# The order of requests in an attention, and the order of the first tiles, in a hybrid decoder block on one Trainium2 core

## What is computed

```python
u = rms_norm(h, norm_w[layer])
proj = jnp.einsum('bsd,dc->bsc', u, w_in[layer])
hg_q, hg_f, hg_i, hg_z, at_q, at_k, at_v, at_z = jnp.split(proj, split_points, axis=-1)
o_hg = hgrn2_mixer(hg_q, hg_f, hg_i, lb)                      # gated linear recurrence
o_hg = rms_norm_per_head(o_hg) * g * silu(hg_z)
q, k = rope(at_q, positions), rope(at_k, positions)
for window, dilation in ((128, 1), (512, 4), (2048, 16)):     # causal, dilated windows
    outs, lses <- dilated_window_attention(q, k, at_v, window, dilation)
o_at = sum(softmax(lses) * outs) * silu(at_z)
h = h + concat([o_hg, o_at]) @ w_out
return rms_norm(h, final_norm_w)
```

## Time and profile before

| | us |
|---|---|
| median of 3 runs (1322.99, 1329.15, 1329.57) | 1329.15 |
| the profiled execution, its own time | 1334.47 |
| its span, first to last instruction | 1332.7 |
| TensorE busy, share of the span | 1278.8, 96% |
| VectorE, ScalarE, GpSimd busy | 702.9, 462.8, 435.6 |

### The profile page before, as it was taken

One profiled execution on the slowest core, in us unless ns is written; L12 is line 12 of the kernel. 1 busy time (PEld: TensorE's weight loads), 2 busy tenths in 40 slices (PEclk: granted clock), 3 DMA queues, 4 the chain that ended last, 5 costly groups with the idle time before them and its releaser, 6 DMA issues.

```text
span 1332.7 us, 23441 instructions
## 1 busy us (share of the span) xinstructions
PE 1278.8 (96%) x8520; PEld 1111.0 (83%) x8520; DVE 702.9 (53%) x1885; ACT 462.8 (35%) x1328; POOL 435.6 (33%) x441
## 2 busy tenths in 40 slices
PE   5999999999999999999999999999999998999997
PEld 5989988999999989999878777877788776878886
DVE  5846776676666668310444544454455445433332
ACT  6721222121222212112445544554555456311111
POOL 5732344232533323030233333333433333202000
PEclk9999999999999999999999999999999999999999
DMA  6520112211121122233355445544554666545431
GB/s 219 157 84 16 58 61 74 72 57 56 56 71 53 61 88 64 61 113 84 83 145 138 121 107 145 138 120 109 152 139 113 163 179 167 168 136 172 143 111 63
DMA packets 121714, 143.89 MB, mean 108 GB/s; under 512 B 20352, under 2 KB 86400, under 8 KB 121600
## 3 DMA queue, kind: packets, MB, share of 16 engines
q1 hardware_dynamic: 119200, 138.46, 36.7%
q10 hardware_dynamic: 2400, 3.93, 1.2%
HBM read 87.56 MB, written 29.62 MB: 88 GB/s over the span
## 4 chain that ended last, share of the span: by engine, by line
PE 79%; DMA 9%; DVE 4%; SPq 2%; issue 2%; POOL 2%; ACT 1%; ACTq 0%; POOLq 0%; DVEq 0%
PE bank L657 11%; PE bank L659 10%; PE bank L658 10%; PE bank L849 4%; PE bank L851 4%; PE bank L850 4%; PE bank L822 4%; PE bank L823 4%; PE bank L821 4%; DMA ks<-turned 3%; PE bank L913 2%; PE bank L982 2%; PE bank L922 2%; PE bank L738 2%; PE bank L975 2%
## 5 line engine op out<-in xcount | busy, mean ns | idle before, releaser
L657 PE MATMUL bank<-w_hi,u_hi 128*128 128x256 f32 x768 | 220.9, 288 | 1.5 <-POOL w_lo L1263 1.0
L659 PE MATMUL bank<-w_hi,u_lo 128*128 128x256 f32 x768 | 217.8, 284 | 0.0
L658 PE MATMUL bank<-w_lo,u_hi 128*128 128x256 f32 x768 | 217.7, 283 | 0.0
L657 PEld LDWEIGHTS bank<-w_hi,u_hi 128*128 128x128 f32 x768 | 147.5, 192 | 3.2 <-DVE u_lo L1442 1.7
L658 PEld LDWEIGHTS bank<-w_lo,u_hi 128*128 128x128 f32 x768 | 147.6, 192 | 0.1
L659 PEld LDWEIGHTS bank<-w_hi,u_lo 128*128 128x128 f32 x768 | 147.5, 192 | 0.1
L1442 DVE TENSOR_TENSOR room<-room 128x256 f32<-128x256 f32 (+6 forms) x386 | 133.7, 394 | 14.7 <-POOL room L1327 7.8
L1442 DVE TENSOR_TENSOR t<-bank,tab 128x512 f32<-128x512 f32 x64 | 42.5, 685 | 134.1 <-DMA tab<-in_rope 68.4
L821 PE MATMUL bank<-u_hi,w_hi 128*128 128x512 f32 x256 | 108.4, 424 | 0.5 <-issue 0.5
L657 PE MATMUL bank<-u_hi,w_hi 128*128 128x512 f32 x256 | 108.1, 422 | 0.6 <-ACT sg_tile L1071 0.6
L1356 POOL TENSOR_TENSOR r<-t,t 64x512 f32<-64x512 f32 x16 | 35.0, 2187 | 219.5 <-DVE w L1716 208.8
(11 more groups left out here) (171 smaller groups left out, 2906.0 us busy)
## 6 DMA issues: line engine op xcount, KB each, us to landing
qd<-turned SPq DMA_DIRECT2D x64, 256.0 KB, 4.8
stage<-in_w_groups SPq DMA_DIRECT2D x44, 256.0 KB, 4.1
room<-in_x SPq DMA_DIRECT2D x16, 512.0 KB, 4.4
values_gates<-vg_tile SPq DMA_DIRECT2D x64, 128.0 KB, 1.7
room<-values_gates SPq DMA_DIRECT2D x16, 512.0 KB, 4.0
tab<-in_rope SPq DMA_DIRECT2D x16, 512.0 KB, 5.7
wide<-mix_weights SPq DMA_DIRECT2D x32, 256.0 KB, 3.9
xr<-in_x SPq DMA_DIRECT2D x16, 512.0 KB, 5.0
```

What stands on the lines that cost most here:

```text
L657: yield nc.tensor.matmul(dst, lhs_hi(k), rhs_hi(k), start=(k == 0), stop=False)
L658: yield nc.tensor.matmul(dst, lhs_hi(k), rhs_lo(k), start=False, stop=False)
L659: last = nc.tensor.matmul(dst, lhs_lo(k), rhs_hi(k), start=False, stop=(k == KT_N - 1))
```

## The change

Six edits. (1) Pieces 2 and 3 of the first projection's weights get a place of their own (`w_raw`, in a half of `w_lo[1]` that is free then), so SyncE asks for all four without a wait, ahead of tiles 2 and 3. (2) TensorE runs 28 transposes of the identity ahead of tile 0 and 12 ahead of tile 1, into a bank that nothing reads then; tile 2 is turned after 16 of the 24 matmuls of the first projection; ScalarE rounds tile t - 2 ahead of the squares of tile t; VectorE makes the low part of tile 0 ahead of its other work of that step. (3) The unit pieces are asked for at i = 0 of blocks 1, 2 and 3, at the head of the step. (4) Output weights are asked for one per step, behind the values of the step, and the first mixed and attended tiles one step earlier, ahead of that step's far statistics. (5) ScalarE issues the gather of keys of head 0 ahead of the gate and the output copies. (6) The mixing weights of the last block are turned between the two halves of tile 3.

```diff
         w_lo = [at(f"w_lo{s}", W_AT + 4096 * s + 2048, [KT_N, GC], F32R) for s in range(2)]
+        w_raw = at("w_raw", W_AT + 4096 + 2048, [KT_N, GC])
...
+        w_first = [sem("w_first2"), sem("w_first3")]
...
+        def first_raw(i):
+
+            return stage[i][:, :, :] if i < 2 else w_raw[:, 2 * (i - 2):2 * (i - 2) + 2, :]
...
             load_piece(0, 1)
+            for i in (2, 3):
+                sp.dma_start(first_raw(i), w_groups[0, :, 2 * i:2 * i + 2, :]).then_inc(w_first[i - 2], 16)
+            load_x(2)
+            load_x(3)
             sp.dma_start(lb_in, lb_logits).then_inc(lb_landed, 16)
             sp.dma_start(g_all, gate_g).then_inc(g_landed, 16)
-            load_x(2)
-            load_piece(0, 2)
-            load_x(3)
-            load_piece(0, 3)
             sp.dma_start(tri, tri_masks).then_inc(tri_landed, 16)
...
                 if i == 0 and n >= 1:
                     load_far_stats(n - 1)
+                if i == 0 and g >= 1 and v + 1 < AT_UNITS:
+                    load_unit_piece(unit_pieces(v + 1)[2 * g - 2])
+                    load_unit_piece(unit_pieces(v + 1)[2 * g - 1])
...
-                if n in (AT_BLOCKS - 3, AT_BLOCKS - 2) and i < 2:
-                    for j in range(2):
-                        load_out_weights(4 * (n - AT_BLOCKS + 3) + 2 * i + j)
                 if T == AT_TILES - 4:
-                    after(z_ready, AT_BLOCKS)
-                    after(comb_stored, 16 * (AT_BLOCKS - 3))
-                    for t in range(2):
-                        load_mixed(t)
-                        load_attended(t)
                     load_residual(0)
...
                     store_output(n - 1)
-                if v + 1 < AT_UNITS and (g, i) in ((1, 2), (2, 0), (2, 3)):
-                    z = ((1, 2), (2, 0), (2, 3)).index((g, i))
-                    load_unit_piece(unit_pieces(v + 1)[2 * z])
-                    load_unit_piece(unit_pieces(v + 1)[2 * z + 1])
+                if n in (AT_BLOCKS - 3, AT_BLOCKS - 2):
+                    load_out_weights(4 * (n - AT_BLOCKS + 3) + i)
+                if T == AT_TILES - 5:
+                    after(z_ready, AT_BLOCKS)
+                    after(comb_stored, 16 * (AT_BLOCKS - 3))
+                    for t in range(2):
+                        load_mixed(t)
+                        load_attended(t)
                 if i == 3:
                     after(e_done, 4 * T + 4)
...
+            def idle_transposes(many):
+
+                for _ in range(many):
+                    nc.tensor.transpose(bank[5][:, 0:P], ident[:, :], ident[:, :])
+
+            idle_transposes(28)
             x_transposes(0)
+            idle_transposes(12)
             x_transposes(1)
             for t in range(TILES):
-                if t + 2 < TILES:
+                if 1 <= t < TILES - 2:
                     x_transposes(t + 2)
                 pe.wait_ge(ulo_done, t + 1)
-                run(phase1_tile(0, t, "prologue"))
+                matmuls = phase1_tile(0, t, "prologue")
+                if t == 0:
+                    run(itertools.islice(matmuls, 16))
+                    x_transposes(2)
+                run(matmuls)
...
-                if t == 3:
-                    turn_weights(AT_BLOCKS - 1)
                 for half in range(1 if t == 1 else 0, 2):
+                    if t == 3 and half == 1:
+                        turn_weights(AT_BLOCKS - 1)
                     for k in range(KT_N):
                         run(output_matmuls(t, half, k))
...
             for step in range(TILES + 4):
+                t = step - 2
+                if 0 <= t < TILES:
+                    act.wait_ge(un_done, t + 1)
+                    nc.scalar.copy(u_hi[:, :, t * P:(t + 1) * P], un[t % 2]).then_inc(uhi_done, 1)
                 if step < TILES:
...
                     nc.scalar.activation(xsq, xt[step % X_SLOTS], ACT.Square,
                                          accum_out=ss[:, step:step + 1]).then_inc(xsq_done, 1)
-                t = step - 2
-                if 0 <= t < TILES:
-                    act.wait_ge(un_done, t + 1)
-                    nc.scalar.copy(u_hi[:, :, t * P:(t + 1) * P], un[t % 2]).then_inc(uhi_done, 1)
...
                     queries_keys_hi(n + 1)
+                if i == 2 and g != 3:
+                    act.wait_ge(qk_lo, n + 2)
+                    gather_keys(nc.scalar, n + 1, (0,))
                 if T == AT_TILES - 3:
...
                         take_output(z)
-                if i == 2 and g != 3:
-                    act.wait_ge(qk_lo, n + 2)
-                    gather_keys(nc.scalar, n + 1, (0,))
...
+            def low_parts(t):
+
+                dve.wait_ge(uhi_done, t + 1)
+                tt(u_lo[:, :, t * P:(t + 1) * P], un[t % 2], u_hi[:, :, t * P:(t + 1) * P].bitcast(F32),
+                   ALU.subtract).then_inc(ulo_done, 1)
...
                 t = step - 1
+                if step == 2:
+                    low_parts(0)
                 if 0 <= t < TILES:
...
                 t = step - 2
-                if t >= 0:
-                    dve.wait_ge(uhi_done, t + 1)
-                    tt(u_lo[:, :, t * P:(t + 1) * P], un[t % 2], u_hi[:, :, t * P:(t + 1) * P].bitcast(F32),
-                       ALU.subtract).then_inc(ulo_done, 1)
+                if t >= 1:
+                    low_parts(t)
```

More of the change, by code:

```diff
@@ L1052, in split_hi @@
             def split_hi(n, i, slot):
-                act.wait_ge(w_landed[i % 2], n * 32 + 16 * (i // 2 + 1))
-                nc.scalar.copy(w_hi[slot][:, 2 * i:2 * i + 2, :], stage[i % 2][:, :, :]).then_inc(hi_done, 1)
+                if not (isinstance(n, int) and n == 0):
+                    act.wait_ge(w_landed[i % 2], n * 32 + 16 * (i // 2))
+                elif i < 2:
+                    act.wait_ge(w_landed[i], 16)
+                else:
+                    act.wait_ge(w_first[i - 2], 16)
+                raw = first_raw(i) if isinstance(n, int) and n == 0 else stage[i % 2][:, :, :]
+                nc.scalar.copy(w_hi[slot][:, 2 * i:2 * i + 2, :], raw).then_inc(hi_done, 1)
             def split_unit_hi(piece):
                 hi, _, raw = dst_of(piece)
-                act.wait_ge(w_landed[piece % 2], 16 * (piece // 2 + 1))
+                act.wait_ge(w_landed[piece % 2], 16 * (piece // 2))
                 nc.scalar.copy(hi, raw).then_inc(hi_done, 1)
@@ L1262, in split_lo @@
                 pool.wait_ge(hi_done, n * 4 + (i + 1))
-                nc.gpsimd.tensor_tensor(w_lo[slot][:, 2 * i:2 * i + 2, :], stage[i % 2][:, :, :],
+                raw = first_raw(i) if isinstance(n, int) and n == 0 else stage[i % 2][:, :, :]
+                nc.gpsimd.tensor_tensor(w_lo[slot][:, 2 * i:2 * i + 2, :], raw,
                                         w_hi[slot][:, 2 * i:2 * i + 2, :].bitcast(F32), ALU.subtract)\
```

## The result

| | before | after |
|---|---|---|
| median of 6 runs, same chip | 1328.84 us (1322.99 to 1335.89) | 1316.45 us (1313.49 to 1318.37) |
| the profiled execution, its own time | 1334.47 | 1318.37 |
| its span | 1332.7 | 1316.6 |
| start of the first HGRN2 matmul | 81.01 | 82.28 |
| from there to the end of the span | 1251.7 | 1234.3 |

The ratio is 0.9912 [0.9888, 0.9937]: 12.4 us faster, where 23.6 were forecast. The direction and the range (1296 to 1317) hold, the size does not. The last two rows already say where to look: between these two executions the prologue, which was to bring 3.7 us, costs 1.3, and the rest brings 17.4.

A forecast was written before the change was run, and what follows sets the result against it. TensorE, busy 1278.8 of 1332.7 us, was taken as the bound, so only its waits and slow-clock work could be won. Terms summed to -23.6: 1310.9 for the profiled execution, 1305.5 for the median; range 1296 to 1317.

The forecast's parts named there:

- part 1: Prologue: tile 1's projection starts at 20.4 instead of 24.13 us, -3.7, if the clock has risen by then.
- part 5: Clock: all four slow stretches at 0.50 lie behind waits that the change removes and go, -6.6.
- part 4: Output weights: far-value waits go, -4.1; queries at steps 56 and 60 come 0.5 late each, +1.0 (bounds 0 and 5).
- the median as the base: Terms read from the profiled execution (1334.47 us) were taken off the median of the runs, 1329.15.
- The prediction's own sign of being wrong: Clock at 0.50 as often as before, or waits at L822 at steps 4 to 12.
- Part 6: First mixed and attended tiles: waits end, -2.9; late far statistics delay step 61's mixing weights, +5.1, with a slow stretch, +1.7.
- Parts 2, 3 and 7: Attention: unit pieces' queries -6.1 and ScalarE's copies of turned weights -2.5; keys -4.3; last mixing weights -1.2.
- the waits only move: Rival: each earlier transfer pushes another, parts 2 to 6 bring a fifth, about -5; 1319 us; chance 0.08.
- transposes do raise the clock: Answers the prologue rival that transposes don't: -3.7 becomes +0.6, 1309.8 us; chance 0.13.
- unit pieces at nine places: Slower rival: 0.5 MB of pieces ahead of far values delays these, +33, net +10, 1339 us; chance 0.03.

The follow-up runs named there:

- f2: The changed kernel run again with no edit: 1315.35 us, ratio 0.9907 to the kernel before.
- f1: The changed kernel with ScalarE's old order (squares ahead of rounding) from tile 3 on, timed: 1313.30 us, ratio 0.9888 to the kernel before.
- e7: The changed kernel with ScalarE's old order (squares ahead of rounding) from tile 3 on, profiled once: 1313.58 us.
- e6: The changed kernel with output weights asked for two at i = 0 and two at i = 1, behind the values; profiled once: 1317.65 us.
- e2: The kernel before with only the attention and output edits (3 to 6): 1315.28 us, ratio 0.9900 to the kernel before.
- e1: The kernel before with only the prologue edits (1 and 2): 1331.82 us, ratio 1.0025 to the kernel before.
- e5: The changed kernel with the far statistics' store ahead of its step's output weight and mixed and attended requests (steps 55, 59); profiled once: 1313.82 us.
- e4: The changed kernel with 64 idle transposes instead of 40, filling TensorE's gaps: 1321.64 us, ratio 0.9945 to the kernel before.
- e8: e4 once more, profiled once: 1316.46 us.
- d2: The changed kernel with ScalarE's old order from tile 3, earlier far statistics' store, output weights moved off i = 2, and e4's transposes: 1314.60 us, ratio 0.9905.

## Why the prediction was right and wrong

What the change does to the transfers was foreseen. Four steps failed: the term of part 1 (-3.7 put, +1.3 measured), that of part 5 (-6.6 put, no slow stretch fewer in the profiled execution), the new price in part 4 (+1.0 put, 5.1 measured), and the median as the base.

**Part 1, the prologue (-3.7): failed; +1.3 in the profiled execution, -0.2 in f2, the same kernel.** Three steps of its working were wrong, and HGRN2's start measures them against the 77.3 that the term meant. First, "the 12 take 1.6 at the upper, in the idle stretch ahead of tile 1", with the first projection costed at full clock: the clock had risen, but TensorE then stood still for 2.01 and 1.12 us, and in six of the eight profiled executions with these 40 transposes it was at 0.50 under the first projection or part of it (worth 1.5 to 1.8 us in the changed kernel and f1, where this lasted 6.83 us; in the other four it lasted 3.41). Second, "ScalarE rounds ahead of the squares" was costed for tile 0 alone; from tile 3 on it delays the squares (2.0 from tile 4 to HGRN2). Third, "today's durations" were taken for VectorE: its scaling at 0.75, its low part at 1.22. The timelines of VectorE and GpSimd after:

```profile
11.35 1.75 DVE L1492 TENSOR_SCALAR room<-room 128x1024 f32<-128x1024 f32 x1 [0.19 <-POOL room L1319]
13.01 2.30 DVE L1465 TENSOR_TENSOR u_lo<-room,u_hi 128x1024 fp32r<-128x1024 f32 x1
15.23 1.27 DVE L1465 TENSOR_TENSOR room<-bank,nw 128x512 f32<-128x512 f32 x2
16.43 1.36 DVE L1492 TENSOR_SCALAR room<-room 128x1024 f32<-128x1024 f32 x1
```
```profile
12.50 1.72 POOL L1286 TENSOR_TENSOR w_lo<-w_raw,w_hi 128x512 fp32r<-128x512 f32 x1
14.31 1.05 POOL L1315 TENSOR_SCALAR room<-room 128x1 f32<-128x1 f32 x1
...
15.96 1.28 POOL L1286 TENSOR_TENSOR w_lo<-w_raw,w_hi 128x512 fp32r<-128x512 f32 x1
```

The pieces that come early put GpSimd's splits right beside VectorE's work: 1.0, 1.1 and 0.6 us more for three operations. No run took this away alone. That it makes up what is left is argued, not shown: with order and clock both right, e7, whose VectorE has the same three long operations, starts tile 1 at 22.26 (20.4 forecast) and HGRN2 at 78.51 (77.3). The sum also left out the norm of tile 1 (15.23), which VectorE does between the low part of tile 0 and the scaling of tile 2; by luck the norm of tile 0 ended 1.3 us earlier than put (11.16 instead of 12.47). The Trainium skill (SBUF — State Buffer, SBUF: two separate sides) says that a GpSimd operation and a VectorE operation with two SBUF inputs, or in a two-port mode, lock a shared pair of ports against each other. The trace agrees: the norm, whose first input lies in PSUM, stays at 1.27 beside the last split (15.23 to 16.50, the split from 15.96), and that split takes 1.28, while the split beside the long scaling takes 1.72.

**Part 5, the clock (-6.6): failed in the profiled execution.** Four slow stretches stand in its attention, as before: three behind the new waits of parts 4 and 6 (1065.96, 1100.09, 1110.33), one at 878.22 behind a wait for keys of 2.0 that the prediction left in place. In f2, the same kernel, there are two. A stretch was counted as belonging to the waits that the change removed; it can come behind any wait of such a size, and need not (see the end). The prediction's own sign of being wrong, the clock at 0.50 as often as before, was met.

**Part 4: removed as said (-4.1), and the new price mis-sized.** The queries at steps 56 and 60 are late by 2.14 and 2.91, 5.1 in all; "0.5 for each" was the wrong end of its own bounds, 0 and 5. In e6, with no output weight ahead of these gathers, the two waits are gone. One request of 512 KB ahead of a gather cost what two of 256 KB had cost.

**Part 6: right in kind.** The far statistics stood 7.17 us behind the loads, and the new wait at the mixing weights of step 61 is there: 3.0 where 5.1 were put, with its slow stretch; the waits for mixed tiles (-2.9) went.

**Parts 2, 3 and 7: right.** Queries at steps 8, 24 and 40 have no wait left; L964's five waits fell from 3.5 to 0.4 (-2.5 forecast); keys went from 9.6 to 4.8 (-4.3 forecast), the three at the heads of units staying; the last mixing weights wait no more.

**The base.** "The sum is taken off the median" was a step of its own, and wrong. Against the execution that it was read from, the attention's forecast of -19.9 comes near: -17.4 in the changed kernel's execution, -21.2 in e2's, -21.1 in f2's. Part of this is luck. From HGRN2 on TensorE's idle time fell by 14.8 us (38.5 to 23.7), where the terms without the clock had 15.0: the queries cost 4.1 more than put, but step 61 cost 2.1 less, and copies and keys brought 1.1 more. Its busy time fell by 2.6 (5.4 in f2), where the clock's terms had 4.9. But the execution before had about 7 us more to remove than e1's, which runs the same attention. Taking waits off a long execution and the sum off a typical one counts luck as gain. So the miss of 10.9 (23.6 forecast, 12.7 from 1329.15 to 1316.45) is 5.0 of prologue, 2.5 of attention, and 3.4 of base, if it is read from these two executions: they differ by 16.1, the medians by 12.7.

**The rivals.** By its number, 1319, "the waits only move" came nearer to the 1316.45 than the forecast did, but not by its mechanism: idle time fell as forecast. None decided: transposes do raise the clock; the waits for queries moved (e6 shows it plainly), and besides them only the statistics that part 6 had named; unit pieces at nine places made no far values late.

## What to carry to other kernels

Read a wait's size from more than one execution before taking it off a median. When a request is moved, look for whoever is asked for next on that queue, in its new place; in a crowded block something stood behind the bytes wherever they were put. And when work is pulled forward, its durations must be read where it lands: beside a busy GpSimd, and under the clock of that place.

## What was not expected of the hardware

Transposes alone raised the clock. In the changed kernel 20 of them took 4.26 us from 3.56 on, 0.21 each, and the other 8 of the 28 took 1.06, 0.13 each, before any matmul on data had run; the record has 1.00 from 7.83. The Trainium skill (TensorE: Matmul & The Clock Gate, Part 4: PE-mode transpose) says that a transpose doesn't count for the clock as a matmul does; for these fp32 transposes the trace says otherwise.

Whether the clock falls behind a given wait is not fixed. At step 56, 2.14 us cost a slow stretch in the changed kernel; 2.45 in f2, the same kernel, and 3.19 in e5 did not. The window in e5:

```profile
1065.48:1068.90 3.42, 3.42 (x21) 3.09 (x22) 2.29 (x8) 1.22 (x4) 0.00 (x0) 1.00 0.53 176
```

In the prologue the clock fell in six of the eight profiled executions with 40 idle transposes, and in none of the three with 64 (e4, e8, d2). The length of the gap ahead of tile 1 does not decide it: 1.76 to 2.02 us in the six, 1.87 and 2.37 in the two that held the clock (e7, f2).

More idle transposes gave longer medians in both pairs, 1321.64 against 1316.45 and 1314.60 against 1310.29, though their profiles start HGRN2 earlier (the first pair stood on two chips; its ratios are 0.9945 and 0.9912). In e4 the long runs have a lower mean clock, in d2 they have not. The cause stays open.
